# The second attention's head norm computed with tokens on partitions, its factors spread by products with the identity

## What is computed

```
    o = o.transpose(1, 0, 2, 3, 4).reshape(b, s, h, 2 * d)
    o = rmsnorm_2(o, subln) * (1.0 - lambda_init)
    return o.reshape(b, s, h * 2 * d)
...
        y = (g[:, :, 0] * (o_a @ w_up_a[l]) + g[:, :, 1] * (o_b @ w_up_b[l])
             + g[:, :, 2] * (o_c @ w_up_c[l]))
        x = x + y @ w_out[l]
```

## Time and profile before

| | us |
|---|---|
| median of 3 runs | 1640.18 |
| lowest and highest run | 1638.62, 1640.49 |
| the profiled execution, its own time | 1638.12 |
| its span, from the first to the last instruction | 1636.1 |
| PE busy in the span | 1562.6 |
| DVE busy in the span | 893.3 |
| ACT busy in the span | 651.5 |

### The profile page before, as it was taken

One profiled execution on the slowest core, in us unless ns is written; L12 is line 12 of the kernel. 1 busy time (PEld: TensorE's weight loads), 2 busy tenths in 40 slices (PEclk: granted clock), 3 DMA queues, 4 the chain that ended last, 5 costly groups with the idle time before them and its releaser, 6 DMA issues.

```text
span 1636.1 us, 25662 instructions
## 1 busy us (share of the span) xinstructions
PE 1562.6 (96%) x10931; PEld 1255.8 (77%) x10931; DVE 893.3 (55%) x1302; ACT 651.5 (40%) x1022; POOL 62.6 (4%) x30
## 2 busy tenths in 40 slices
PE   8998989889989999999999999999999999999998
PEld 7886434434435349988889799999989889899998
DVE  6933212112111148667887576647566879576654
ACT  2034112112201126454764554435454664464443
POOL 0000000000000000024000000000007000000000
PEclk9988999999999999999999999999999999999999
DMA  9165999999999995626334566474634543265550
GB/s 350 49 252 206 417 428 428 428 428 429 429 429 427 427 402 199 206 104 199 136 117 142 165 196 197 165 259 157 210 122 156 180 155 130 85 215 190 181 205 28
DMA packets 126913, 393.79 MB, mean 241 GB/s; under 512 B 4320, under 2 KB 60000, under 8 KB 114016
## 3 DMA queue, kind: packets, MB, share of 16 engines
q1 hardware_dynamic: 126816, 392.38, 63.5%
HBM read 386.34 MB, written 1.05 MB: 237 GB/s over the span
## 4 chain that ended last, share of the span: by engine, by line
PE 73%; DVE 12%; DMA 10%; ACT 2%; issue 1%; SPq 0%; DVEq 0%; ACTq 0%
PE psum L1259 11%; PE psum L990 10%; PE psum L991 10%; PE psum L993 10%; DMA ring<-w 8%; PE psum L1324 4%; DVE outs L1984 3%; PE psum L1596 2%; PE psum L1594 2%; DVE w_lo L636 2%; PE psum L1597 2%; PE psum L1222 2%; PE psum L1417 1%; PE psum L1418 1%; PE psum L1416 1%; PE psum L951 1%
## 5 line engine op out<-in xcount | busy, mean ns | idle before, releaser
L990 PE MATMUL psum<-h_parts,w_hi 128*128 128x256 f32 x1472 | 358.2, 283 | 0.1
L991 PE MATMUL psum<-h_parts,w_lo 128*128 128x256 f32 x1472 | 352.5, 279 | 0.0
L636 DVE TENSOR_TENSOR w_lo<-raw_a,w_hi 128x1024 fp32r<-128x1024 f32 x184 | 221.9, 1222 | 114.7 <-ACT w_hi L1616 114.0
L990 PEld LDWEIGHTS psum<-h_parts,w_hi 128*128 128x128 f32 x1472 | 276.3, 188 | 6.1 <-issue 5.4
L991 PEld LDWEIGHTS psum<-h_parts,w_lo 128*128 128x128 f32 x1472 | 277.2, 188 | 0.2
L1616 ACT ACTIVATE w_hi<-raw_a 128x1024 fp32r<-128x1024 f32 x202 | 210.4, 1055 | 160.1 <-PE psum L993 62.7
L993 PE MATMUL psum<-h_parts,w_hi 128*128 128x256 f32 x1472 | 201.9, 279 | 0.0
L1259 PE MATMUL psum<-ring,outs 128*64 128x512 f32 x720 | 167.2, 621 | 26.0 <-DMA ring<-w 24.8
L993 PEld LDWEIGHTS psum<-h_parts,w_hi 128*128 128x128 f32 x1472 | 184.7, 188 | 0.0
L1259 PEld LDWEIGHTS psum<-ring,outs 128*64 128x64 f32 x720 | 58.5, 143 | 132.0 <-issue 132.0
L1616 ACT ACTIVATE w_hi<-raw_b 128x1024 fp32r<-128x1024 f32 x100 | 104.8, 1056 | 90.4 <-PE psum L993 52.7
(11 more groups left out here) (310 smaller groups left out, 2535.0 us busy)
## 6 DMA issues: line engine op xcount, KB each, us to landing
ring<-w SPq DMA_DIRECT2D x76, 2048.0 KB, 16.4
raw_a<-w_in SPq DMA_DIRECT2D x20, 2048.0 KB, 7.9
raw_a<-w_gu SPq DMA_DIRECT2D x32, 1024.0 KB, 7.8
raw_b<-w_in SPq DMA_DIRECT2D x10, 2048.0 KB, 8.9
wp<-w SPq DMA_DIRECT2D x8, 2048.0 KB, 18.7
hs<-w SPq DMA_DIRECT2D x8, 2048.0 KB, 23.1
raw_b<-w_gu SPq DMA_DIRECT2D x12, 1024.0 KB, 7.6
raw_a<-w_down SPq DMA_DIRECT2D x8, 1536.0 KB, 6.6
```

Of the source, the lines that this page charges most:

```text
L636: return eng.tensor_tensor(chunk_part(w_lo, n), chunk_raw(n), chunk_part(w_hi, n).bitcast(F32), ALU.subtract)
L990: mm(to, hi[:, k, :], h_hi[:, k, :], start=(k == 0), stop=False)
L991: mm(to, lo[:, k, :], h_hi[:, k, :], start=False, stop=False)
```

## The change

The sums are made the other way around: a 128 x 128 piece of the squares (128 channels of a head by 128 tokens) is the weight, and two columns of the mean matrix stream past it. The result has tokens on partitions and one column for each head and half of the tokens, doubled: 16 columns. Root and reciprocal are taken of these 16 columns (`sub_roots`). To bring the factors back to channels on partitions, a new step `subln_factors` makes for each of the 16/2 columns a product in which that column, repeated 128 times, is the weight and the identity streams past: each of 128 channels gets the row of 128 factors. These 8 products write the duo that the sums were in, so it stays in use until DVE has read the factors from there. The new step stands behind `up 16` and `gate_last`; `subln_rest` is gone, and the one `w_lo` and split of C0 now stand ahead of the root.

```diff
-        + [("subln_sums",), ("apply", 23), ("outs_high", 2), ("outs_low", 2), ("subln",), ("subln_rest",), ("up", 16, 0),
-           ("gate_last",), ("outs_high", 1), ("outs_low", 1), ("up", 17, 2), ("up", 18, 1)]
+        + [("subln_sums",), ("apply", 23), ("outs_high", 2), ("outs_low", 2), ("subln",), ("up", 16, 0),
+           ("gate_last",), ("subln_factors",), ("outs_high", 1), ("outs_low", 1), ("up", 17, 2), ("up", 18, 1)]
...
-        for _ in range({"subln_sums": used + PARTS - split, "subln_rest": 1}.get(w[0], 0)):
+        for _ in range({"subln_sums": used + PARTS - split, "subln": 1}.get(w[0], 0)):
...
+        sub_roots = sq[:, 4, 0:16]
...
-                        for k in range(4):
-                            last = mm(view(duo("subln"), 0, 4, SEQ)[:, k, :], c("mean_sub"), sq[:, k, :],
-                                      start=True, stop=True)
+                        for t in range(TT):
+                            for k in range(4):
+                                at = (t * 4 + k) * 2
+                                last = mm(duo("subln")[:, at:at + 2], sq[:, k, t * P:(t + 1) * P], c("mean_sub")[:, 0:2],
+                                          start=True, stop=True)
                         last.then_inc(sums_done, 1)
+                    elif kind == "subln_factors":
+
+                        pe.wait_ge(subln_ready, l * 2 + 1)
+                        for t in range(TT):
+                            for k in range(4):
+                                at = (t * 4 + k) * 2
+                                last = mm(view(duo("subln"), 0, 4, SEQ)[:, k, t * P:(t + 1) * P],
+                                          sub_roots[:, at:at + 1].broadcast_to([P, P]), ident, start=True, stop=True)
+                        last.then_inc(subln_turned, 1)
...
-                        f(sq[:, 4:8], view(duo("subln"), 0, 4, SEQ), ACT.Sqrt, bias=eps[:]).then_inc(std_ready, 1)
+                        f(sub_roots, duo("subln")[:, 0:16], ACT.Sqrt, bias=eps[:]).then_inc(std_ready, 1)
...
-                            act_e.wait_ge(subln_ready, l + 1)
+                            act_e.wait_ge(subln_ready, l * 2 + 2)
...
                         v.wait_ge(std_ready, l * 4 + 2)
+                        v.reciprocal(sub_roots, sub_roots).then_inc(subln_ready, 1)
+                    elif kind == "subln_factors":
+                        v.wait_ge(subln_turned, l + 1)
+                        v.scalar_tensor_tensor(outs[:, 1], outs[:, 1], lam[:, 3:4], view(duo("subln"), 0, 4, SEQ),
+                                               ALU.mult, ALU.mult).then_inc(subln_ready, 1)
+                        v.wait_ge(subln_ready, l * 2 + 2)
                         v.sem_inc(free_of("subln"), 1)
-                        link(v.reciprocal(sq[:, 4:6], sq[:, 4:6]))
-                    elif kind == "subln_rest":
-                        link(v.reciprocal(sq[:, 6:8], sq[:, 6:8]))
-                        v.scalar_tensor_tensor(outs[:, 1], outs[:, 1], lam[:, 3:4], sq[:, 4:8], ALU.mult, ALU.mult
-                                               ).then_inc(subln_ready, 1)
```

More of the change, by code:

```diff
@@ L239, in with_splits @@
             low = []
-        held = w[0] in ("gates", "probs", "scores", "turn", "apply", "cross_q", "square_b", "sums", "evac", "rope", "index_product", "subln_sums", "outs_high", "outs_low", "subln", "subln_rest") or (w[0] == "exp" and w[1] >= 24)
-        for _ in range({"subln_sums": used + PARTS - split, "subln_rest": 1}.get(w[0], 0)):
+        held = w[0] in ("gates", "probs", "scores", "turn", "apply", "cross_q", "square_b", "sums", "evac", "rope", "index_product", "subln_sums", "outs_high", "outs_low", "subln", "subln_factors") or (w[0] == "exp" and w[1] >= 24)
+        for _ in range({"subln_sums": used + PARTS - split, "subln": 1}.get(w[0], 0)):
             out += [("split", split), ("low", split)]
@@ L529, in build @@
          lam_dot, lam_exp, rot_even, rot_odd, rope_tmp, rope_ready, idx_raw, wi_turned, idx_done, relu_ready, selneg_ready,
-         scores_done, rowmax_ready, exp_ready, probs_ready, probsT_done, probsT_ready, attn_done, subln_ready,
+         scores_done, rowmax_ready, exp_ready, probs_ready, probsT_done, probsT_ready, attn_done, subln_ready, subln_turned,
          direct_done, chunk_used, w_hi_ready, w_lo_ready, w_lo_pool_ready, act_hi_ready, act_lo_ready,
@@ L544, in build @@
             "lam_dot lam_exp rot_even rot_odd rope_tmp rope_ready idx_raw wi_turned idx_done relu_ready selneg_ready "
-            "scores_done rowmax_ready exp_ready probs_ready probsT_done probsT_ready attn_done subln_ready "
+            "scores_done rowmax_ready exp_ready probs_ready probsT_done probsT_ready attn_done subln_ready subln_turned "
             "direct_done chunk_used w_hi_ready w_lo_ready w_lo_pool_ready act_hi_ready act_lo_ready "
```

## The result

The changed kernel took 1648.33 us (median of five runs, 1645.03 to 1649.52), the kernel before 1639.7 beside it (five runs, 1638.12 to 1640.49): a ratio of 1.0049, 95% interval 1.0034 to 1.0064. That is +8.6 us where +1.5 was predicted, above the range given and above 0.2%. The profile after is of an execution of 1648.33, its span is 1646.3.

What follows compares the result with a forecast made beforehand. DVE was taken to set the end, with at most 1.44 us a layer for PE to regain. Per layer +1.9 factors, -0.1 sums, -0.2 C3, -0.85 wait gave +0.75, so 1640.18 + 1.5 = 1641.7 us, range 1639.4 to 1644.0.

Steps and rivals of the forecast that it cites:

- The sums: Norm sums on PE: eight two-column products take 1.81 us instead of 1.90, gain 0.1 a layer; surroundings and waits unchanged.
- Half price: Rival: the factors cost as the first block's, 0.080 an instruction, 1.4 us a layer, time 1640.7; chance 0.12.
- The factors: New PE step between A3 and C0: 16 instructions at 0.113 plus 0.1, 1.9 us a layer; ends 1.4 and 3.9.
- that rival, 3.8: Rival: load and stream of the factors add up, 0.232 an instruction, 3.8 us a layer, time 1645.5; chance 0.12.
- What comes back: Behind the factors, PE's gap before C3 closes (0.2 us a layer) and its wait before `out 19` shrinks (0.85).
- The wait before `out 19`'s second half: PE's wait for DVE's row at the stretch's end: 0.4 us instead of 1.24, with DVE later by 0.75.
- s: How much later PE is after the norm step: 1.9 - 0.1 = 1.8 us.
- The collision with POOL: DVE's L2417 stays at 2.2 us beside POOL; rival: POOL misses it, 0.36 us a layer, 1640.9, chance 0.10.
- the free relief: Rival: DVE's 6.4 us come off and PE's addition hides, at most 2.9 us, time 1637.3; chance 0.03.
- The sum of these: Per layer +1.9 factors, -0.1 sums, -0.2 C3, -0.85 wait before `out 19`: +0.75 us, +1.5 for both.

Runs made afterwards that it cites:

- e2: The kernel before with only the sums changed to eight products of two columns, the norm left out of the result: 1640.13 us, ratio 1.0005.
- e3: The changed kernel without the eight factor products, DVE multiplying by what lies in the buffer: 1640.2 us, ratio 1.0002.
- e13: The changed kernel, sums still two columns wide, with factors made by eight transposes in place of sixteen product instructions: 1643.53 us, ratio 1.0022.
- e1: The changed kernel with its eight sums streaming 128 columns instead of 2: 1646.3 us, ratio 1.0041.
- e5: e1 with the factors made by eight transposes in place of sixteen product instructions: 1639.28 us, ratio 0.9998.
- e8: e1 run again with nothing edited, for a second profiled execution: 1642.02 us.
- e4: The kernel before without its two reciprocals of 512 columns, nothing else altered: 1636.69 us, ratio 0.9981.
- e14: The kernel before with root and reciprocal in one ACT pass over 1024 columns, both DVE reciprocals gone: 1636.79 us, ratio 0.9976.
- e7: e1 with the sixteen factor instructions run twice in each layer: 1643.66 us, ratio 1.0024.
- e6: e1 with the four old sums, 1.90 us of PE, in the place of the factors: 1644.95 us, ratio 1.0033.

## Why the prediction was wrong

**The sums: the step that failed.** It took the eight narrow products as 1.81 us in place of 1.90, "Gain 0.1 us a layer", and went on: "What comes before and behind them on PE, and the waits there, are as they were." The term is right to 0.05, 1.85 from 835.13 to 836.98. What failed is the second sentence: behind them the clock falls, and A0 takes longer. All five profiles with narrow sums in the two layers (after twice, e2, e3, e13) show a fall behind them in both; of the thirteen with wide sums none does. (In the first block, whose sums are narrow in every kernel, 13 of the 18 profiles show it, so it needn't come each time.) In after it costs 1.1 us in the first layer (63.08 against e1's 62.0) and 2.6 to 2.8 in the second, 3.8 in all. In the medians the width comes to 4.25 (e13 against e5) and to 2.0 (after against e1). The row was at hand: in the earlier trace rows, taken for the price of an instruction, the eight products L951 behind the narrow sums go from 108.11 to 111.04, 0.37 apiece, where 256 columns cost 0.2375. In e5's profile, which has no fall there, they take 0.2375 too (111.21 to 113.11). The table by stretch of before says why, and below it stand the same products and the factors of the first block in e5:

```profile
108.90:111.00 2.10, 2.10 (x6) 1.21 (x4) 0.06 (x1) 2.04 (x3) 0.00 (x0) 0.50 0.00 0
...
111.21 1.97 PE L952 MATMUL psum<-big,ring 128*128 128x256 f32 x8
113.11 1.97 PE L943 MATMUL psum<-consts,wp 128*64 128x128 f32 x32
115.01 3.29 PE L952 MATMUL psum<-big,ring 128*128 128x256 f32 x14
```

The same fall, which lasts until 112.3, is in the price of the rival "Half price": the 32 instructions took 0.080 each partly at half the clock; in e5 it is 0.059 (113.11 to 115.01).

**The cover that went away.** The prediction saw that DVE ends last and counted what comes back with it. It did not see the other side: DVE's row also covered what PE loses. Under the old reciprocals a single fall cost 0.2 and 0.5 us (e2); without them a single one cost 1.5 and a double one 3.0 (e3).

**The factors**: 1.9 forecast, 1.70 plus 0.08 on the product behind (0.36 for 0.28) measured, 1.78. Load and stream don't add up, so that rival, 3.8, is out: 0.106 an instruction, where the two-column products with the same loads took 0.116 and a stream of 128 columns is 0.119 by the prediction's halving. The Trainium skill, TensorE: Matmul & The Clock Gate, section The mechanism, lets a load overlap only where the row groups differ (the prediction names the section behind it); the trace of the factors, 0.106 with all 128 rows, speaks against that, as L1491's did. PE doesn't wait before the factors, and ACT's root pushes no split.

**What comes back**: C3 has no gap, as forecast. The wait before `out 19`'s second half is 0.72 in place of 0.4: counted from A0, PE came to it later by 1.36 (39.96 us in e8, 38.60 before), not 1.6, and DVE to its last term by 0.85 (37.33 and 36.48), not 0.75. By the prediction's own terms this wait does not depend on how long the factors hold PE (s, by which PE is later, falls out of 1.24 + (s - 1.05) - (s - 0.2)), and so it is: 0.7 in e4 and e14, which add nothing to PE, in e5 and in e7. The whole relief came out as summed, 0.2 + 0.85 = 1.05 forecast and 1.05 in e4, but partly by luck: the wait gave 0.52 in place of 0.85, and small delays at C3 and at the start of `out 19` gave 0.31 and 0.21 where 0.2 was counted. The collision with POOL stayed, so that rival is out too, and so is the free relief.

**The sum of these** is right where the clock holds: e1's stretch is 0.8 to 0.9 us longer than that of before's first profile in each layer, in four profiles, and 0.6 to 0.75 longer than that of its second; after's sums are 0.1 shorter. Forecast was 0.75. So of 8.6 us the forecast's mechanism carries about 1.6 and the falls behind the narrow sums about 3.8. Without those falls the time would be some 1644.5, still above the range, and e1, which lacks them, took 1646.3: the failed step is not the whole of the miss. The remaining 3 us lie outside the changed stretch. Time at half the clock can be 2 of them at most: after has 73.1 us of it in the mean, before 58.9, and of these 14.2 us some 10 lie behind the sums. In the two profiles of each kernel, after has 1.1 us more from layer 1's `cross_k` to layer 2's sums, 0.7 more in the rest, and 1.3 more ahead of the first sums, where nothing was changed and executions differ by up to 4. Why after, e1 and e6 have more falls in cross attention than before, and e7, e4 and e14 fewer, stays open: the falls there change from one execution to the next, and two profiles of a kernel don't settle it. How much of this is the change's doing stays open with it. A version with the narrow sums moved into dense work was not tried. One slip of the prediction has no part in this: by its own terms its range begins at 1639.7 (1640.7 less 1), not at 1639.4.

## What to carry over

Where a full PE is given a row of tiny products, ask what clock the dense work behind them gets, and look for a place in the trace where the same form already stands: the products behind it tell by their own duration. Taking work from the engine that ends last also takes the cover from all that is late on the other; here a fall that had cost 0.2 to 0.5 us cost 1.1 to 1.5 without that cover. And where the gain is capped by a wait of a us or so, a relief that puts nothing on PE (e14) is the one that gets it.

## What was not expected of the hardware

The granted clock fell with PE busy for 6.42 of the 7.00 us ahead, 1.85 of them in products of two columns; in all the falls seen it is 0.50, and dense products of 256 columns then take 0.21 apiece in place of 0.117. Over 160 executions of eleven kernels, each less its stretch's own difference at full clock, time and time at half the clock go together with a correlation of 0.85 (0.66 when each kernel's own mean is taken off first). And ACT's reciprocal root over 1024 columns takes 1.12 us with no further table load, where root and reciprocals together took 1.1 on ACT and 6.7 on DVE.
